# Latent stage on the unscaled residual: the root of the token norm moved to the evictions of the next feed-forward stage

## What is computed

```
def rmsnorm(x, g):
    y = x * rsqrt(mean(x * x, -1) + 1e-6)
    return y * g

def swiglu(u, wg, wu, wd):
    return (silu(u @ wg) * (u @ wu)) @ wd

h = h + 0.5 * swiglu(rmsnorm(h, ffn_post_norm[0]), ...)      # ffn1
# kv: keys and values shared by the later attention
kv_a  = rmsnorm(h, kv_in_norm) @ w_dkv                       # 1024 -> 128 + 64
c_kv  = rmsnorm(kv_a[..., :128], ckv_norm)
k_rope = apply_rope(kv_a[..., 128:], cos, sin)
h = h + 0.5 * swiglu(rmsnorm(h, ffn_pre_norm[1]), ...)       # ffn2
h = h + mla_attention(rmsnorm(h, mix_norm[1]), c_kv, k_rope) # mla
```

## Time and profile before

| | us |
|---|---|
| median of 3 runs | 1905.34 (1904.9 to 1905.36) |
| the profiled execution, its own time | 1906.39 |
| span in its trace | 1904.6 |
| TensorE busy | 1879.5 |
| VectorE / ScalarE / GpSimd busy | 1230.9 / 945.5 / 70.8 |
| chain of work that ended last: PE / DVE / ACT / POOL | 81% / 4% / 3% / 1% |

### The profile page before, as it was taken

One profiled execution on the slowest core, in us unless ns is written; L12 is line 12 of the kernel. 1 busy time (PEld: TensorE's weight loads), 2 busy tenths in 40 slices (PEclk: granted clock), 3 DMA queues, 4 the chain that ended last, 5 costly groups with the idle time before them and its releaser, 6 DMA issues.

```text
span 1904.6 us, 34293 instructions
## 1 busy us (share of the span) xinstructions
PE 1879.5 (99%) x13518; PEld 1749.6 (92%) x13518; DVE 1230.9 (65%) x1646; ACT 945.5 (50%) x1296; POOL 70.8 (4%) x95
## 2 busy tenths in 40 slices
PE   9999999999999999999999999999999999999998
PEld 8999899999998989999999998899999998889998
DVE  6666666675556647666766689666676665877665
ACT  5443544454446645444544458644454446455443
POOL 0001100000000000000100000100010001010000
PEclk9999999999999999999999999999999999999999
DMA  7554454545553135555555442565545453344552
GB/s 286 198 196 169 151 214 185 195 164 201 198 188 143 68 138 197 198 196 199 199 198 187 155 144 98 207 237 197 184 164 209 185 200 122 131 148 174 197 198 100
DMA packets 61505, 338.83 MB, mean 178 GB/s; under 512 B 6976, under 2 KB 7360, under 8 KB 33024
## 3 DMA queue, kind: packets, MB, share of 16 engines
q1 hardware_dynamic: 59472, 330.00, 46.9%
q0 software_dynamic: 1968, 7.93, 1.2%
HBM read 336.85 MB, written 1.05 MB: 177 GB/s over the span
## 4 chain that ended last, share of the span: by engine, by line
PE 81%; DVE 4%; ACT 3%; issue 1%; POOL 1%; DVEq 0%; ACTq 0%; POOLq 0%
PE X L1650 48%; PE Y L1650 32%; DVE arena L1438 1%; ACT hiA L586 1%; DVE loA L1091 1%; ACT arena L795 0%; PE X L1688 0%; DVE xs L1163 0%; DVE h L1170 0%; ACT xh L632 0%; PE X L1674 0%; PE Y L2132 0%; DVE arena L1375 0%; DVE xl L1123 0%; PE X L1690 0%
## 5 line engine op out<-in xcount | busy, mean ns | idle before, releaser
L1650 PE MATMUL X<-xh,hiA 128*128 128x256 f32 x2480 | 684.1, 277 | 1.2 <-DVE xl L1123 0.8
L1650 PE MATMUL X<-xl,hiA 128*128 128x256 f32 x2480 | 682.2, 277 | 0.0
L1650 PE MATMUL X<-xh,loA 128*128 128x256 f32 x2480 | 673.7, 277 | 0.0
L1091 DVE TENSOR_TENSOR loA<-rawA,hiA 128x2048 fp32r<-128x2048 f32 x218 | 499.4, 2291 | 266.3 <-ACT hiA L586 265.9
L1650 PEld LDWEIGHTS X<-xh,hiA 128*128 128x128 f32 x2480 | 465.8, 188 | 2.8 <-DVE loA L1077 1.2
L1650 PEld LDWEIGHTS X<-xl,hiA 128*128 128x128 f32 x2480 | 466.3, 188 | 0.0
L1650 PEld LDWEIGHTS X<-xh,loA 128*128 128x128 f32 x2480 | 460.4, 188 | 0.0
L586 ACT ACTIVATE hiA<-rawA 128x2048 fp32r<-128x2048 f32 (+1 forms) x235 | 423.5, 1802 | 50.0 <-PE Y L1650 30.3
L1650 PE MATMUL Y<-hiB,act_hh 128*128 128x512 f32 x704 | 275.4, 391 | 2.6 <-DVE act_hl L1237 2.6
L700 ACT ACTIVATE act_s<-act_s 128x256 f32<-128x256 f32 x154 | 64.3, 417 | 429.4 <-DVE act_s L1224 429.4
L1650 PE MATMUL Y<-hiB,act_hl 128*128 128x512 f32 (+1 forms) x880 | 275.8, 346 | 0.0
(11 more groups left out here) (256 smaller groups left out, 2199.4 us busy)
## 6 DMA issues: line engine op xcount, KB each, us to landing
rawA<-in_wa SPq DMA_DIRECT2D x221, 1024.0 KB, 5.4
rawB<-in_wb SPq DMA_DIRECT2D x181, 512.0 KB, 3.5
row_gain<-in_rows POOLq DMA_DIRECT2D x8, 512.0 KB, 6.6
arena<-in_gla POOLq DMA_DIRECT2D x1, 1280.0 KB, 5.9
h<-in_x SPq DMA_DIRECT2D x2, 512.0 KB, 4.5
arena<-in_pool POOLq DMA_DIRECT2D x1, 768.0 KB, 5.5
arena<-in_taps POOLq DMA_DIRECT2D x1, 576.0 KB, 5.7
rawA<-in_wa SPq DMA_DIRECT2D x2, 256.0 KB, 6.3
```

What stands on the lines that cost most here:

```text
L1091: nc.vector.tensor_tensor(loA[p][:, :], rawA[p][:, :], hiA[p][:, :].bitcast(f32), ALU.subtract).then_inc(a_lo, 1)
L1650: return say(nc.tensor.matmul(*args, **kw))
```

## The change

`kv` becomes a raw stage that stands early, and `ffn2` becomes `late`: it works on unscaled tokens and multiplies the root in at its evictions, as the other feed-forward stages do. In detail:

- `following` turns the first token block ahead of the last quarter of `ffn1`'s last down product, by plain transposes; `diag` and its two VectorE instructions go away, as does GpSimd's eps addition of this stage.
- The squares of the tokens, before four halves ahead of the transposes on ScalarE, become two whole squares behind the last `oh`, ahead of `latent_square`.
- The first weight tile of the latents is multiplied with all high tokens of slots 0 to 3 first, then with their low parts.
- `latent_eps` now adds eps to the two token sums, waits until GpSimd has made both token roots, and then makes the latents' eps term from the unscaled token sum; only then can GpSimd make the latents' root.
- `latent_roots` spreads the two token roots too (two more matmuls), behind the wait for the latents' root.
- The rope keys are added up first (one 128x256 addition) and multiplied by the root later, behind `latent_norm`.
- Every step of `ffn2` has two more VectorE multiplications (gate and up by `root`), and Silu reads the scaled gate from SBUF.

```diff
-        late = kind == "ffn" and not reuse
-        raw = late or kind in ("mla", "gla")
+        late = kind == "ffn"
+        raw = late and not reuse or kind in ("kv", "mla", "gla")
@@ ScalarE, latent and the start of ffn
             def latent(s):
-                norm_in(s)
                 xt_hi(s, "kv", range(6))
                 second_hi(s, "ffn2", range(4))
                 xt_hi(s, "kv", (6, 7))
                 split_A(s["a"] + 2, (s["a"] + 2) % 2)
                 second_hi(s, "ffn2", range(4, KD))
+                token_square(s, 0)
+                token_square(s, 1)
...
-                        if s["late"]:
-                            act.wait_ge(root_psum, s["deferred"] + 1)
-                            nc.scalar.activation(root, Y[:, 0, 0:TOKENS], ACT.Copy).then_inc(root_done, 1)
+                        act.wait_ge(root_psum, s["deferred"] + 1)
+                        nc.scalar.activation(root, Y[:, 0, 0:TOKENS], ACT.Copy).then_inc(root_done, 1)
@@ VectorE
+                    if first:
+                        dve.wait_ge(root_done, s["deferred"] + 1)
+                    dve.wait_ge(gate_psum, e + 1 + f)
+                    nc.vector.tensor_tensor(act_s[:, p, :], gate, root, ALU.mult
+                                            ).then_inc(gate_scaled, 1)
+                    dve.wait_ge(up_psum, e + 1 + f)
+                    nc.vector.tensor_tensor(act_h[:, p, :], up, root, ALU.mult).then_inc(up_scaled, 1)
                     if first and s["reuse"]:
                         latent_norm()
+                        latent_rotated()
...
             def latent(s):
-                norm_in(s)
                 xt_lo(s, "kv", range(4))
...
             def latent_eps(s):
-                n = s["norm_mid"]
+                n, token = s["norm_mid"], s["norm"]
+                for t in range(TT):
+                    add_eps(token + t, s["square"] + t + 1, halves=False)
+                dve.wait_ge(rstd_done, token + TT)
                 dve.wait_ge(kv_var, 1)
-                nc.vector.tensor_scalar(ms_eps[:, n:n + TT], Y[:, 0, 0:2 * TT:2], EPS, None, ALU.add).then_inc(kv_eps, 1)
+                nc.vector.scalar_tensor_tensor(ms_eps[:, n:n + TT], ms_eps[:, token:token + TT], EPS, Y[:, 0, 0:2 * TT:2],
+                                               ALU.mult, ALU.add).then_inc(kv_eps, 1)
@@ TensorE
                 def latent_roots():
 
+                    pe.wait_ge(rstd_done, plan[plan.index(s) - 1]["norm_mid"] + TT)
+                    for t in range(TT):
+                        token = plan[plan.index(s) - 1]["norm"] + t
+                        ins = mm(Y[:, 0, P * t:P * t + P], rstd[:, token:token + 1].broadcast_to([P, P]),
+                                 ident[:, :], start=True, stop=True)
+                    ins.then_inc(root_psum, 1)
                     n = plan[plan.index(s) - 1]["norm_mid"]
                     pe.wait_ge(rstd_done, n + TT)
...
             def latent(s):
-                transposes(s, 0)
-                transposes(s, 1)
+                first_transposes(s)
...
+                for k in range(4):
                     for q in range(3):
+                        if (k, q) == (0, 1):
+                            transposes(s, 1, (1,))
+                        if q == 0:
+                            pe.wait_ge(xh_done, KD * s["xt"] + k + 1)
+                        sl = slice(P * q, P * q + P)
+                        mm(latent_bank(q), wh[:, k, sl], xh[:, k, :], start=k == 0 and q < 2, stop=False)
+                        mm(latent_bank(q), wl[:, k, sl], xh[:, k, :], start=False, stop=False)
+                for k in range(4):
+                    wait_x(s, k)
+                    for q in range(3):
+                        mm(latent_bank(q), wh[:, k, P * q:P * q + P], xl[:, k, :], start=False, stop=False)
```

More of the change, by code:

```diff
@@ L67, in stage_plan @@
         early = raw and bool(before) and not crossed and before["kind"] in ("ffn", "mla")
-        opened = late and bool(plan)
+        opened = late and not reuse and bool(plan)
         s = dict(at, kind=kind, i=i, name=name, second=second, reuse=reuse, late=late, raw=raw, ahead=ahead,
@@ L77, in stage_plan @@
         s["norm_post"] = s["norm_mid"] + mid
-        s["square_mid"] = at["square"] + pre * (1 if late else 2)
+        s["square_mid"] = at["square"] + pre * (1 if late or kind == "kv" else 2)
         s["square_post"] = s["square_mid"] + (0 if kind == "kv" else mid)
@@ L482, in _ @@
                 before_mixer = {"ffn1": ("mla",), "final": ("hyb",), "ffn5": ("gla",)}.get(s["name"], ())
-                if s["late"]:
+                if s["late"] and not s["reuse"] or s["kind"] == "kv":
                     powers(s["norm"], s["norm"] + 2)
@@ L1210, in ffn @@
                     latent_eps(plan[plan.index(s) - 1])
-                if s["late"] and not halved:
+                if not s["reuse"] and not halved:
                     for t in range(1 if s["opened"] else 0, TT):
@@ L1883, in gate_up @@
                         pe.wait_ge(prod_done, e - 1 + f)
[L1884 removed]
+                    block_of(f, p, 0, (latent_roots if s["reuse"] else roots) if fresh else None)
                     if fresh and a == 0:
@@ new lines, in latent @@
+                for k in range(4):
+                    wait_x(s, k)
+                    for q in range(3):
+                        mm(latent_bank(q), wh[:, k, P * q:P * q + P], xl[:, k, :], start=False, stop=False)
+                owed.append(a_free)
+                n = s["a"] + 1
+                wait_A(n)
+                wh, wl = bank_view(hiA[n % 2], 4, 512), bank_view(loA[n % 2], 4, 512)
+                for q in range(3):
+                    for r in range(4):
+                        if q == 0:
+                            wait_x(s, 4 + r)
+                        sl = slice(P * q, P * q + P)
+                        ins = by_weights(latent_bank(q), wh[:, r, sl], wl[:, r, sl], 4 + r, False, r == 3 and q != 1)
+                    if q != 1:
+                        ins.then_inc(kv_psum, 1)
```

68 lines of the change are left out of this document (24 added, 44 removed).

## The result

The changed kernel is slower: its median over 11 executions is 1910.22 us (1908.43 to 1912.41), that of 11 executions of the kernel before 1905.58 (1904.9 to 1907.53), a ratio of 1.0023 with a 95% interval of 1.0015 to 1.0031. Measured again beside other runs of the kernel before, on another occasion, the ratio was 1.0018 (1.0009 to 1.0027). I had forecast 1907.3 with a range from 1905.5 to 1909.2.

A forecast was written before the change was run, and what follows sets the result against it. TensorE bounds the kernel (busy 1879.5 of 1904.6 us), with a ScalarE-VectorE-GpSimd-TensorE chain deciding this stretch. Terms -2.3 + 2.08 + 1.57 + 0.45 + 0.2 = +2.0 us on median 1905.34 forecast 1907.3, range 1905.5 to 1909.2.

The forecast's parts named there:

- C: Start of `ffn2`: token powers on GpSimd join the chain ahead of the latents' power, +1.57 us (bounds +0.4 and +4.1).
- the two of near 1 us ahead of it: Early `ffn2`: TensorE waits near 1 us for `latent_square`, and near 1 us for the second weight tile's low part.
- D: Two more root matmuls on TensorE, with nothing beside them to hide the time: +0.45 us (0.36 to 0.47).
- E: Two more VectorE multiplications per `ffn2` step: nothing in the loop, +0.2 us at the last step (0 to 0.3).
- A: End of `ffn1` into `kv`: plain transposes start earlier, so the last `oh` comes 2.3 us sooner (-2.1 to -2.5).
- B: Two whole token squares on ScalarE between the last `oh` and `latent_square`: +2.08 us, with no slack to hide it.
- the rival with the powers held: Token powers fall under a long VectorE subtraction, the pair taking 3.72 us: end at 1909.8, chance 0.06.
- The rival with the shorter chain: Token powers back to back, latents' power past GpSimd before the subtraction: C near +0.4, total +0.8, 1906.2, chance 0.12.
- the cover: Gate and up work behind the root matmuls hides the first split product's preparation: 5.3 against 5.95 us, 0.6 to spare.
- the warnings I had listed: Roots before 415.8: C wrong; after 418.5: GpSimd held; `ffn2`'s loop longer than 164 us: E wrong.

The follow-up runs named there:

- e2_squares: Changed kernel with the two token squares moved between the second and third of the last four `oh`: 1906.89 us, ratio 1.0005.
- e8_free: e3_both with VectorE waiting for the latents' root before the low part of the first `loB`: 1904.58 us, ratio 0.9991.
- e12_free: The kernel of e8_free measured again on another occasion: 1904.84 us, ratio 0.9992.
- e1_filled: Changed kernel with 20 idle transposes just ahead of the wait for the latents' root: 1907.77 us over nine executions, ratio 1.0010.
- e3_both: e2_squares with the two token eps also moved ahead of `latent_keys` on VectorE: 1904.16 us, ratio 0.9994.
- e11_after: The changed kernel as it is, measured again beside other runs of the kernel before: 1909.75 us, ratio 1.0018.

## Why the prediction was wrong, point by point

The direction of the sum was right and its places were too, but the measured time lies 1 us above my range. (The two ends that I gave the sum, +0.5 and +5.0, were added up wrongly: the bounds of the terms make +0.3 and +4.9.) The step that failed is in C, where I wrote "after a gap of some 2.5 us on TensorE instead of 0.78" and priced that gap, and the two of near 1 us ahead of it, by their length alone. That they can lower the granted clock for the work behind them stood neither in the sum nor among the rivals. With all gaps filled and the schedule unmoved, the kernel measured 1907.1, near my 1907.3, and its ratio 1.0009 is +1.7 us. The changed kernel's two ratios are +4.4 and +3.4. The difference of 1.7 to 2.7 us is the missing term; each ratio is uncertain by about 1.7 us, so its size is rough.

Not all of it need be lost behind these gaps. Seen falling there is the clock of one execution, by 1.6 us. And kernels without the three gaps also measure more than their traces say: e2_squares by 1.9 us, e8_free by 1.6 and e12_free by 1.1, where the changed kernel has 3.1 and 1.8 and the filled ones 0.8 and -0.4 (the median's difference from the kernel before, less what the trace shows up to the end of `ffn2`). Where those three lose it stays open.

The steps, from the mark, in traces without loss of clock in this stretch (e1_filled for D and E):

| step | forecast | measured |
|---|---|---|
| A, last `oh` | -2.3 | -2.42 (12.44 against 14.86) |
| B, squares | +2.08 | +2.08 (0.34 ahead at the second tile's high part); again by e2_squares |
| C, token roots | +1.57 | +1.37 at the roots; 1.35 by e3_both |
| D, two more matmuls | +0.45 | +0.45 (0.92 against 0.47, in e1_filled) |
| E, end of `ffn2` | +0.2 | +0.17 (1.48 at the end, 1.31 at the first down) |
| the rows of gate and up behind the roots | none | -0.17 (4.86 against 5.03) |
| sum | +2.0 | +1.5 |
| clock behind the gaps | none | 1.6 in the first trace, 0 in that of e11_after |

A: plain transposes 0.11 us each, sixteen of them, and the wait of 0.6 for `xh`, as in `mla`. The Trainium skill's factor of 4 (TensorE: Matmul & The Clock Gate, Terms), against which I had gone by the rows, would have given 0.9 us more, and no such time is there.

C: the pair took 1.09 us instead of 1.23, which was a pair with a wait inside it, and GpSimd followed the eps by 0.24 instead of 0.30. VectorE waited, and so the rival with the powers held did not come about. That its 1909.8 lies near the measured time is chance: in the trace no power is longer than its forecast.

E: twenty downs of `ffn2` take 164.01 us, with the two multiplications in them:

```profile
423.43:587.44 164.01, 164.01 (x1223) 155.18 (x1222) 102.06 (x122) 72.22 (x81) 0.00 (x0) 1.00 0.52 194
```

The rival with the shorter chain was wrong on the changed kernel, since the latents' power took 1.55 beside the subtraction. But its mechanism exists: e8_free made the power 0.70. The last split product was ready 4.67 us behind the roots' start (5.3 forecast), so the cover held. The roots started 0.3 us earlier than forecast, and none of the warnings I had listed came true. I had no warning for the clock in the list.

## What to carry to other kernels

A gap on the engine that bounds the kernel can cost more than its length, in some executions and not in others: before you accept a longer wait there, look in the trace at the granted clock of the rows behind it, in more than one execution. If the gap can't be removed, idle matmuls in it can help: with 36 transposes in the three gaps the ratio was lower by 1.7 to 2.7 us of time, a size that these runs give only roughly. When a step moves from one engine's idle time into a chain through three engines, sum along the chain, and look for the idle time of the engine elsewhere in the same stage: the two squares cost 2.08 us behind the last `oh` and nothing two instructions earlier, where ScalarE waited anyway. A busy share can't show a halved clock, since the engine counts as busy for twice as long.

## What the runs showed of the hardware

- The granted clock behind the same gaps of 0.9, 0.8 and 2.3 us was at 0.50 for some 3 us in one execution and at 1.00 in another of the same kernel. With idle transposes in the gaps it stayed at 1.00 there in both traces, and 1 of 20 executions had a mean clock below 0.999, against 18 of 22 with the gaps open.
- A single gap of 2.0 us, in the same place of every program, was followed by such a fall in 6 of the 12 traces that have it.
- GpSimd's power on two columns takes 0.70 us with VectorE idle (e8_free) and 1.55 with a 1.22 us subtraction of two SBUF inputs started ahead of it. The Trainium skill (SBUF — State Buffer, Who interferes with whom) says that such an instruction keeps GpSimd's reads out for its length; the two rows agree.
- Small unused multiplications on GpSimd took 0.14 us each behind one another (seven of them 1.97 us in all, three 1.40), less than I had assumed by a factor of three.
